# Two attentions with probabilities turned three units behind their scores, first halves made ahead, and one program block

## What is computed

```python
# first block: 8 query heads of 64 in two groups, two branches (selected blocks and window) that share
# the form of a causal softmax attention; each branch has its own keys and values
sw = q @ k.T * scale;  p_w = softmax(where(causal, sw, NEG));  o_w = p_w @ v
o = g[..., 0:1] * o_c + g[..., 1:2] * o_s + g[..., 2:3] * o_w
# third layer: 16 heads of 64, with a forget gate summed into the logits
logits = qi @ k.T + (ci[:, None] - c[None, :])
p = softmax(where(key_pos <= qpos, logits, -inf))
o = (p @ v) * sigmoid(g)
return o @ w_out
```

## Time and profile before

| | us |
|---|---|
| median of 3 runs | 2178.94 |
| lowest, highest | 2178.33, 2182.07 |
| the profiled execution, its own time | 2175.64 |
| its span, first to last instruction | 2173.6 |
| first attention, first scores to end of value products | 151.5 to 236.2 |
| second attention, the same | 1638.6 to 1731.0 |
| mean granted clock of TensorE over the span | 0.985 |

### The profile page before, as it was taken

One profiled execution on the slowest core, in us unless ns is written; L12 is line 12 of the kernel. 1 busy time (PEld: TensorE's weight loads), 2 busy tenths in 40 slices (PEclk: granted clock), 3 DMA queues, 4 the chain that ended last, 5 costly groups with the idle time before them and its releaser, 6 DMA issues. The chain is left out here.

```text
span 2173.6 us, 26059 instructions
## 1 busy us (share of the span) xinstructions
PE 2078.8 (96%) x9944; PEld 1677.8 (77%) x9944; DVE 1221.4 (56%) x1719; ACT 795.9 (37%) x1235; POOL 21.2 (1%) x45
## 2 busy tenths in 40 slices
PE   7898899999999999999999999999998899999997
PEld 6765678888888888877788888778785578888885
DVE  5567645455445355456575574764436657647465
ACT  4237343332222132245343342442327734324242
POOL 0000000000000000000000000000000000000000
PEclk9999999999999999999999999999999999999998
DMA  4510322232222322321122222223220022222221
GB/s 162 158 59 1 107 68 78 96 113 96 96 97 84 109 97 77 122 91 59 58 97 97 97 85 109 76 79 107 89 85 1 20 97 78 97 97 96 97 82 54
DMA packets 34237, 188.48 MB, mean 87 GB/s; under 512 B 4440, under 2 KB 8696, under 8 KB 14400
## 3 DMA queue, kind: packets, MB, share of 16 engines
q1 hardware_dynamic: 31296, 179.41, 23.4%
q0 software_dynamic: 1696, 5.72, 1.0%
q10 hardware_dynamic: 1152, 2.10, 0.3%
HBM read 182.54 MB, written 2.11 MB: 85 GB/s over the span
## 5 line engine op out<-in xcount | busy, mean ns | idle before, releaser
L337 ACT ACTIVATE w_hi<-w_raw 128x2048 fp32r<-128x2048 f32 (+3 forms) x174 | 314.4, 1807 | 824.3 <-PE bank L405 696.2
L403 PE MATMUL bank<-a_hi,w_hi 128*128 128x512 f32 x1376 | 539.5, 392 | 3.9 <-DVE shared L2539 1.7
L405 PE MATMUL bank<-a_hi,w_lo 128*128 128x512 f32 x1376 | 535.7, 389 | 0.0
L404 PE MATMUL bank<-a_lo,w_hi 128*128 128x512 f32 x1376 | 535.5, 389 | 0.0
L351 DVE TENSOR_TENSOR w_lo<-w_raw,w_hi 128x2048 fp32r<-128x2048 f32 (+3 forms) x174 | 374.9, 2156 | 141.3 <-ACT w_hi L337 141.2
L403 PEld LDWEIGHTS bank<-a_hi,w_hi 128*128 128x128 f32 x1376 | 258.5, 188 | 60.1 <-issue 3.9
L405 PEld LDWEIGHTS bank<-a_hi,w_lo 128*128 128x128 f32 x1376 | 258.3, 188 | 53.9
L404 PEld LDWEIGHTS bank<-a_lo,w_hi 128*128 128x128 f32 x1376 | 258.4, 188 | 53.3 <-issue 0.3
L403 PE MATMUL bank<-big_halves,w_hi 128*128 128x512 f32 x616 | 240.6, 391 | 3.1 <-DVE w_lo L351 3.0
L404 PE MATMUL bank<-big_halves,w_hi 128*128 128x512 f32 x616 | 239.7, 389 | 0.0
L405 PE MATMUL bank<-big_halves,w_lo 128*128 128x512 f32 x616 | 239.7, 389 | 0.0
(11 more groups left out here) (323 smaller groups left out, 2445.9 us busy)
## 6 DMA issues: line engine op xcount, KB each, us to landing
w_raw<-in_w_fu SPq DMA_DIRECT2D x44, 1024.0 KB, 4.8
w_raw<-in_w_up SPq DMA_DIRECT2D x16, 1024.0 KB, 4.8
w_raw<-in_w_down SPq DMA_DIRECT2D x16, 1024.0 KB, 4.8
w_raw<-in_w_fd SPq DMA_DIRECT2D x16, 1024.0 KB, 4.8
w_raw<-in_w_fd SPq DMA_DIRECT2D x8, 768.0 KB, 4.3
w_raw<-in_w_rqk SPq DMA_DIRECT2D x4, 1024.0 KB, 5.2
w_raw<-in_w_rvg SPq DMA_DIRECT2D x4, 1024.0 KB, 4.9
w_raw<-in_w_gate SPq DMA_DIRECT2D x4, 1024.0 KB, 4.8
```

Of the source, the lines that this page charges most:

```text
L337: act.activation(w_hi[slot][:, cols], raw[slot][:, cols], ACT.Copy).then_inc(hi_half_ready.sem if half == 0 else hi_ready.sem, 1)
L403: pe.matmul(out, w[0], x[0], start=first, stop=False)
L404: pe.matmul(out, w[0], x[1], start=False, stop=False)
L405: return pe.matmul(out, w[1], x[0], start=False, stop=last)
```

## The change

- Turning stands at step s for unit s - 3 (before: s - 2), values for s - 4, so copying on ScalarE is three units behind too. There are three sets of probabilities (`prob`, with two more tiles each), maxima and sums.
- All units are written out; the loops over turns are gone. The next pair's splitting stands at the first unit of a pair on both engines: ahead of copying and exponentials on ScalarE, behind the maxima on VectorE.
- `begin_act` and `begin_dve` split the first pair (and the first attention's keys) during the third block of the projection ahead, into halves that nothing else uses then (`fx_first` in the second attention). Scores of units 0 and 1 wait only for the evacuation of the banks that they write.
- In the second attention the order of the two projections is `fg`, `fq`; a dummy exponential (`begin_exp`) stands behind the first splitting. Everything is one program block. The output tiles are split by `split_high` and `split_low`, of which VectorE does seven ahead of its last product with the gate (`ends`).
- TensorE's wait for the end of the first attention stands behind the third row tile of `rvg`, which is written out for that.

```diff
...
-            f.update(fk=(4, [(KT, 256)]), ff=(1, [(KT, 128)]), fv=(4, [(4, 512)]), fq=(4, [(KT, 256)]), fg=(4, [(KT, 256)]),
+            f.update(fk=(4, [(KT, 256)]), ff=(1, [(KT, 128)]), fv=(4, [(4, 512)]), fg=(4, [(KT, 256)]), fq=(4, [(KT, 256)]),
...
+            a_plain = sb(same, "a_plain", [P, KT, S])
...
+            fx_first = sb(same, "fx_first", [P, 4, S], F32R)
...
-        neg_max, row_sum = ([sb(top, f"{n}{r}", [P, 2]) for r in range(2)] for n in ("neg_max", "row_sum"))
+        neg_max, row_sum = ([sb(top, f"{n}{r}", [P, 2]) for r in range(3)] for n in ("neg_max", "row_sum"))
...
+                if spec.blocks == 2 or between:
+                    for b in range(spec.blocks):
+                        use(b, b % 2)
...
+            def prob(u, e):
+                return probs[2 * (u % 3) + e]
...
             def tensor(pe):
-
-                pe.wait_ge(evacuated.sem, b_e)
-                pe.wait_ge(rows_out.sem, b_ro)
-                pe.wait_ge(cmp_dve.sem, b_cd)
...
+                    if u < 2:
+
+                        pe.wait_ge(evacuated.sem, b_e - 1 + u)
                     if i == 0:
-                        pe.wait_ge(staged.sem, b_st + once + c * (2 * each) + (p * each + each))
+                        pe.wait_ge(staged.sem, b_st + once + each * (n + 1))
+                    if u >= 2:
+                        pe.wait_ge(probs_ready.sem, b_p + 2 * (u - 1))
...
-                def step(c, s, unit):
-                    for lead, part in ((0, score), (2, turn), (3, values)):
-                        if unit(lead) and (part is not values or unit(lead)[1] % TT == TT - 1):
-                            part(*unit(lead))
-                over_turns(pe, 3, step)
+                def step(s, unit):
+                    if unit(0) is not None:
+                        score(unit(0))
+                    if unit(3) is not None:
+                        turn(unit(3))
+                    if last_of(unit(4)):
+                        values(unit(4))
+                steps(5, step)
...
+            def begin_dve(dve):
+                if static:
+                    for p in range(2):
+                        k = held[p][1]
+                        dve.wait_ge(high_staged.sem, b_hi + p + 1)
+                        dve.tensor_tensor(k[1], k_of(p), k[0].bitcast(F32), ALU.subtract).then_inc(staged.sem, 1)
+                stage_low(dve, 0)
...
+                    if ends is not None and n == pairs - 1:
+                        ends(dve)
+                    dve.wait_ge(out_ready.sem, b_o + n + 1)
+                    finish(dve, n, out_bank[0 if together else p]).then_inc(out_done.sem, 1)
...
+                def step(s, unit):
+                    if unit(0) is not None:
+                        maximum(unit(0))
+                        if s % U == 0 and s // U + 1 < pairs:
+                            stage_low(dve, s // U + 1)
+                    if unit(1) is not None:
+                        weigh(unit(1))
+                    if last_of(unit(5)):
+                        take(unit(5))
+                steps(6, step)
+
+            def stage_high(act, n):
+                if n == 1:
+                    act.wait_ge(evacuated.sem, b_e)
+                elif n >= 2:
+                    act.wait_ge(scores_ready.sem, b_s + U * (n - 1))
+                for st, src in stagings(n):
+                    act.activation(st[0], src, ACT.Copy).then_inc(high_staged.sem, 1)
...
+            def begin_act(act):
...
+                stage_high(act, 0)
...
+                def step(s, unit):
+                    if s % U == 0 and unit(0) is not None and s // U + 1 < pairs:
+                        stage_high(act, s // U + 1)
+                    if unit(3) is not None:
+                        copy(unit(3))
+                    if unit(0) is not None:
+                        exponential(unit(0))
+                        if not static and s % U == 0:
+                            stage_values(s // U)
+                steps(4, step)
...
                     outputs_copied(dve)
+                    begin_dve(dve)
...
+                elif b == 2:
+                    begin_act(act)
...
-            stages = [{"gpsimd": transfers, "scalar": split_act, "vector": split_dve, "tensor": lambda pe: pe.wait_ge(out_done.sem, b_done)}]
+            stages = [{"gpsimd": transfers, "scalar": split_act, "vector": split_dve}]
...
-            stages.append(dense_rows("rvg", evac_dve=rows_dve, late_dve=rvg_late))
+            stages.append(dense_rows("rvg", evac_dve=rows_dve, late_dve=rvg_late,
+
+                                     between={(0, 2): lambda pe: pe.wait_ge(out_done.sem, b_done)}))
...
-                        stages.append(dense("fq", two_chunks(a_tiles), scaled_to(qT, float(FD) ** -0.5), tile_ready=ready))
-                        stages.append(dense("fg", two_chunks(a_tiles), gates_dve, none, none, gates_act))
-                        run(*before, *stages)
...
-                    run(attention(FH // 4, lambda c, p: qT[:, bass.ds(c * 2 + p, 1), :], lambda c, p: kT[:, bass.ds(c * 2 + p, 1), :],
-                              lambda c, p: v[:, :, bass.ds(c * (2 * P) + p * P, P)], False, (a_hi, a_lo), None, finish, False, fx_probs_t, (sel, parts)))
...
+                        stages.append(dense("fg", two_chunks(a_tiles), gates_dve, none, none, gates_act, tile_ready=ready))
...
+                def split_high(act):
+                    for k in range(KT):
+                        act.wait_ge(out_done.sem, b_done + k + 1)
+                        act.activation(a_hi[:, k, :], gT[:, k, :], ACT.Copy).then_inc(split_hi_done.sem, 1)
+
+                def split_low(dve, tiles):
+                    for k in tiles:
+                        dve.wait_ge(split_hi_done.sem, b_hi + k + 1)
+                        dve.tensor_tensor(a_lo[:, k, :], gT[:, k, :], a_hi[:, k, :].bitcast(F32), ALU.subtract).then_inc(split_lo_done.sem, 1)
...
+                    fx_probs_t, sq + y_part + [a_plain[:, r, :] for r in (4, 5)], (evacuated.n + 4, rows_out.n, cmp_dve.n), key_bias,
+                    lambda dve: split_low(dve, range(KT - 1)))
+
+                def begin_exp(act):
+                    begin_act(act)
+
+                    act.activation(warm[:, :], warm[:, :], ACT.Exp)
...
+                stages.append(dense("fq", two_chunks(a_tiles), scaled_to(qT, float(FD) ** -0.5), begins(begin_dve), none, begins(begin_exp)))
+                stages += [attend, {"scalar": split_high, "vector": lambda dve: split_low(dve, [KT - 1])}]
...
```

286 lines of the change are left out of this document (127 added, 159 removed).

## The result

| | us |
|---|---|
| before, median of 5 runs beside it (lowest, highest) | 2178.94 (2175.65, 2183.1) |
| after, median of 5 runs (lowest, highest) | 2142.32 (2141.06, 2143.88) |
| ratio, with its 95% interval | 0.9828 [0.9817, 0.9838] |
| the profiled execution of after, its own time | 2142.03 |
| its span | 2140.2 |

The kernel became 36.6 us faster. The prediction was 2154 us, from 2147 to 2168: the direction was right, the size was not, and the time lies 4.7 us under the range. In the two profiled executions the spans differ by 33.4 us (2173.6 − 2140.2).

The account below looks back on a forecast made before the run. It took a loop of waits between TensorE, VectorE and ScalarE in the attentions as the bound. Seams of 8.8 us plus 15.5 us by the lag made 24.3 us, from 2178.94 to 2154 us, range 2147 to 2168.

Parts of the forecast that it names:

- The bound by TensorE: Both attentions: TensorE, VectorE and ScalarE wait for one another in a loop; TensorE stands still 11.97 and 11.95 us.
- the lag: Inside both attentions: turning three units behind scores removes waits for weighing; 8.0 and 7.5 us, together 15.5 us.
- The seams: The beginning and end of each attention, four places where TensorE's waits shrink; together 8.8 us.
- third: End of the first attention: TensorE's wait moves to the next stage's third row tile; 1.1 us.
- fourth: End of the second attention: output tiles split early, so TensorE goes straight on after the value products; 1.9 us.
- the sum: Whole kernel: 8.8 us at the seams plus 15.5 us by the lag, 24.3 us, giving 2154 us; chance 0.60.
- second seam: Start of the second attention: sigmoid, splitting and table load covered, no block change; first exponential 3.9 us earlier.
- The most that this can give is all of TensorE's standing still outside the tail: Upper bound on the lag's gain inside the attentions: 9.5 us in the first, 9.6 us in the second.
- the first rival: Scores then wait for exponentials two units back; lag gives half (2162 us, chance 0.14) or nothing (2170 us, 0.13).
- more than the sum: TensorE's clock stays up at the seams (4.9 us) and all idle time goes: 32.8 us at most; chance 0.07.
- first seam: Start of the first attention: first pair split during the projection's third block; first exponential 1.9 us earlier.
- Slower than before: Start of each pair: splitting and value products stand in one row, pairs grow 14.2 us; 2184 us, chance 0.06.

Follow-up runs that it names:

- lag_only: The kernel after with all four seams taken back to before's; lag, third set, written-out loops and the splitting's place kept: 2156.28 us, ratio 0.9887 to before.
- exp_early: The kernel after plus a dummy exponential behind the early splitting of the first attention, moving its table load: 2141.55 us, ratio 0.9822 to before.
- after_again: The kernel after, unchanged, run once more on the same chip: 2142.32 us, ratio 0.9828 to before.
- tensor_alone: The kernel after without maxima, exponentials, weighing, copying, staging of values and all waits for them; output not the reference's: 2122.65 us in one run.
- split_third: The kernel after with the next pair's splitting at the third unit of a pair instead of the first, on both engines: 2141.18 us, ratio 0.981 to before.
- no_lag: The kernel after with turning back at two units behind the scores; three sets, written-out loops and seams kept: 2171.08 us, ratio 0.9954 to before.
- two_sets: The kernel after, turning still three units behind, but with two sets of probabilities, maxima and sums instead of three: 2195.36 us in one run.
- both: The kernel after with VectorE's taking of a pair's output one unit later and only the second pair's splitting moved to the second unit: 2135.98 us, ratio 0.9792.

## Why the prediction was off

**The bound by TensorE**: right in kind. The loop of waits through weighing is what the lag broke; `lag_only` shows it alone.

**The seams**: right up to the first exponential and behind the last value product. First 1.95 us (forecast 1.9), second 4.0 (3.9), third 1.2 (1.1), fourth 1.95 (1.9). Each was worked out from one chain in the time line. What the sum did not have is the 1.9 us that the second seam gives behind its first exponential (`lag_only` against after). Of the table load the sum took the row's 1.28 us and not the 2.66 us that the Trainium skill (ScalarE: Activation LUTs, What ACT_TABLE_LOAD costs) would give with its drain. The row stands: `exp_early` took the load away and gained 1.40 us.

**The lag**: mechanism right, size wrong, 15.5 us forecast; 23.6 measured inside, 21.7 of them without the seams (`lag_only`). The step that failed is the sentence "The most that this can give is all of TensorE's standing still outside the tail". It puts a fall of TensorE's busy time at nothing. Inside the attentions, counted as in the table, TensorE's idle time fell by 8.0 and 5.5 us (11.96 to 3.93 and 11.90 to 6.43), together 13.5 and less than the 15.5 forecast. Its busy time fell by 3.9 and 6.3 us (71.08 to 67.23 and 78.97 to 72.68), together 10.1, and this is where the surplus lies. The second attention's values of after are those of `after_again`, which has all its matmul records there. The sentence was wrong in two ways.

- It took busy time for work. `tensor_alone` measured a need 8.1 and 7.3 us smaller than the busy time. Most of the fall is waits that the profile counts as busy. The rest is the clock: some 1.4 us in pair 4 of the first attention and, by an estimate from before's 1.92 us at 0.50 behind the first exponential (1640.08 to 1642.00), up to 1 us in the second. I had 77.05 busy us for 588 matmuls and no row for what they take by themselves; the sum of the spacings between their starts in a stretch without waits would have told.
- It left the tail out of the idle time that could go, "since the tail's chain (exponential, weighing, turning, copying, values) stays as it was". The chain stayed, but with one turning more between the last scores and the last turning, TensorE had work where it had waited 1.57 and 1.51 us; after's waits for weighing are 0.3 us in all. That is 1.2 to 1.3 us in each attention. The wait for the last copy, 0.86 us, did stay.

That the gain is near the larger slack doesn't mean that no new wait came: scores wait 1.2 and 4.0 us for exponentials, as the first rival said, but for a tenth to a half of what was removed, not for all. I had named that rival's loop and priced it at half or all of the gain; it decided only between 9.75 and 9.15 us a pair.

**The rival "more than the sum"** was the one that came true, with a chance of 0.07 and a sum of 32.8 us at most against 36.6. It put the surplus at the clock in the seams and at all of the idle time, and not at TensorE's need, so its number came nearest without its reason. In the first seam the clock was not won: the same stretch as in the earlier trace rows has a granted clock of 0.51 where it had 0.53. In the second it was, 1.00 for 0.56. The two stretches of after:

```profile
151.50:158.00 6.50, 5.43 (x29) 3.60 (x30) 4.63 (x13) 4.75 (x18) 0.00 (x0) 0.51 0.02 4
...
1618.00:1621.40 3.40, 2.01 (x22) 1.43 (x24) 3.10 (x7) 2.10 (x7) 0.00 (x0) 1.00 0.00 0
```

**"Slower than before"**: refuted. The pairs fell by 1.4 to 1.5 us at full clock, where I had written "about 1 us". The splitting ahead of a pair's first exponentials did cost something: `split_third`, without it, has pairs of 9.50 and not 9.75 us in the second attention, 0.25 us and not the 1.15 that I feared.

**A slip in the first rival.** The "2.3 and 3.0 us" of idle time not put down to weighing are counted in two ways. Without the tail's wait for the last copy (0.86) they are 1.4 and 3.0 us, with it 2.3 and 3.85. Nothing in the sum hangs on it.

**The base.** I took the gain from the median, 3.3 us above the profiled execution. But the 36.6 us between the medians and the 33.4 us between the spans differ by about as much again. Before's runs in this study go from 2172.9 to 2185.1 us, after's from 2141.1 to 2145.2. A part of such a spread is clock falls inside the attentions, as in pair 4 of before's first; that fewer waits make fewer of them would fit after's smaller spread, but no run shows it by itself. So of the 12.3 us between the sum of 24.3 and the 36.6, 6.2 are the lag, 1.9 the start of the second attention, 0.3 the seams as counted, and 0.7 elsewhere. The rest, about 3 us, is that the profiled execution of before was one of its faster ones.

Not settled: how the 1.9 us divide between the clock and the scores made ahead; why `no_lag` waits longer for weighing than before does, beyond the 0.05 to 0.2 us a pair of the splitting's place, and why some of its runs lie near 2168 and others near 2175 us. No run separates the written-out loops from the third set there.

## What to carry to other kernels

- Where an in-order engine waits in a loop with two others, its slack is the stretch minus what its instructions need without waits, and not minus its busy time. Take that need from a stretch of the trace that has no waits, or from a kernel in which the other engines' work is left out; here the whole slack of the first attention was 19.4 us, of which the profile showed 12.0 as idle.
- One more unit of lag pays only with one more set of buffers (2142 against 2195 us here, the latter in one run), and it also took 1.2 to 1.3 us off the wait in the tail.
- When the loop is broken, look for work for which nobody waits ahead of work for which somebody does. Moving a 0.68 us operation by one step gave 0.5 to 0.6 us in each pair that had waited for it.

## What the runs showed of the hardware

- TensorE's granted clock fell inside an attention whose waits are short, not only behind a long gap. In before, the 2 us from 182 (columns as in the earlier trace rows), and the turning there; the two waits of TensorE ahead of the fall are 1.05 us (at 179.57) and 0.47 us:

```profile
182.00:184.00 2.00, 2.00 (x10) 1.67 (x11) 1.83 (x7) 1.17 (x5) 0.00 (x0) 0.50 0.00 0
...
181.74 1.97 PE L1184 MATMUL bank<-const_sb,work 128*128 128x128 f32 x8 [0.47 <-DVE work L1236]
```

  0.50 is the lower level, 1.2 GHz; eight turnings take 1.97 us there and 1.09 at 1683.17. With TensorE alone the granted clock was 1.00 over both attentions, and `two_sets`, with the most waiting, had means of 0.85 and 0.95 over them, before 0.94 and 0.98.
- A table load costs its 1.28 us where it stands on ScalarE's path, and nothing where ScalarE waits behind it. In `both` no copy stands between it and the first splitting, and the first exponential waits for its maximum (the load, and the exponential):

```profile
143.75 1.28 ACT L1296 ACT_TABLE_LOAD   x1
...
152.60 0.37 ACT L1296 ACTIVATE work<-bank,neg_max 128x128 f32<-128x128 f32 x1 [7.57 <-DVE neg_max L1230]
```
